# A whole two-block network on one core: raw first products, moved side work, more expert buffers, and constant products in TensorE's waits

## The reference, cut to what matters

```python
# first block (x: 512 x 1024)
h = rms_norm(x, norm_mix)
proj = h @ w_in                                # 1024 -> about 15,600 columns, split for four branches and their gates
ys = [mamba2_branch(...), rglru_branch(...), retention_branch(...), rwkv7_branch(...)]
merged = sum(sigmoid(gate_m) * (ys[m] @ w_branch[m]) for m in range(4))
x = x + merged @ w_out
h = rms_norm(x, norm_ffn)
u = causal_dwconv(h @ ffn_up)                  # 1024 -> 2 * 2816
x = rms_norm(x + (silu(gt) * val) @ ffn_down, norm_final)
# second block: modulated norms of x and of a context (256 tokens), with six vectors from c @ w_mod
#   gated delta net in both directions + neighbourhood attention, one input and one output projection
#   x = x + gate1 * (concat(gdn, attention) @ w_out_2)
# 16 experts, each takes the 64 tokens with the highest router score:
p = softmax(modulated(rms_norm(x)) @ w_router)
for e in range(16):
    tok = top_64(p[:, e])
    y_e = (silu(h[tok] @ w_gate[e]) * (h[tok] @ w_up[e])) @ w_down[e]    # three 1024 x 1024 matrices
    x[tok] += gate2 * p[tok, e] * y_e
out = rms_norm(x, final_norm_2)
```

## Time and profile before

| | us |
|---|---|
| median of 3 runs | 3022.27 (3018.67 to 3022.57) |
| the profiled execution | 3020.42 |
| its span in the trace | 3018.6 |
| PE busy | 2852.8 (95%) |
| DVE, ACT, POOL busy | 1529.3, 674.6, 713.0 |
| granted TensorE clock, mean | 0.983 of full |

### The profile page before, as it was taken

The page is one execution under the profiler, slowest core; times in us unless marked ns, Lnnn a source line. Parts: engine busy times, 40 slices in busy tenths (PEclk is TensorE's granted clock), DMA queues, the critical chain, the costliest instruction groups (busy, mean ns, idle before and its releaser), DMA issues. The chain is left out here.

```text
span 3018.6 us, 53749 instructions
## 1 busy us (share of the span) xinstructions
PE 2852.8 (95%) x22652; PEld 2048.3 (68%) x22652; DVE 1529.3 (51%) x2561; ACT 674.6 (22%) x1196; POOL 713.0 (24%) x523
## 2 busy tenths in 40 slices
PE   9999999998999989899999999999889997999998
PEld 5854866896788578758688888677768744443432
DVE  5765737445655567645577753764555322111112
ACT  2133022003333334311111100321454211110111
POOL 1212122110888346412122100111257300000000
PEclk9999999999999999999999999999999998999999
DMA  4243223331667100033222223233200047999996
GB/s 171 84 144 105 87 78 112 99 94 59 209 239 256 39 11 4 4 136 92 84 84 84 84 77 91 91 95 91 67 20 4 23 175 283 378 409 409 409 409 266
DMA packets 128477, 426.83 MB, mean 141 GB/s; under 512 B 14945, under 2 KB 22753, under 8 KB 127985
## 3 DMA queue, kind: packets, MB, share of 16 engines
q1 hardware_dynamic: 125936, 412.92, 38.8%
q0 software_dynamic: 2304, 10.49, 1.0%
HBM read 414.09 MB, written 5.06 MB: 139 GB/s over the span
## 5 line engine op out<-in xcount | busy, mean ns | idle before, releaser
L960 PE MATMUL ps<-arena 128*128 128x256 f32 x5376 | 1179.4, 381 | 18.1 <-PEq L911 6.8
L960 PEld LDWEIGHTS ps<-arena 128*128 128x128 f32 x5376 | 1016.3, 191 | 189.2 <-issue 34.7
L891 POOL TENSOR_TENSOR arena<-arena 128x512 f32<-128x512 f32 x90 | 122.4, 1360 | 629.5 <-DMA arena<-in_w_in 293.7
L897 POOL TENSOR_TENSOR arena<-arena 128x512 f32<-128x512 f32 x90 | 114.7, 1274 | 552.7 <-PE ps L960 552.7
L1111 ACT ACTIVATE arena<-ps 128x256 f32<-128x256 f32 x96 | 36.7, 382 | 890.0 <-PE ps L960 507.6
L4200 PE MATMUL ps<-arena 128*64 128x512 f32 x1024 | 224.7, 594 | 10.8 <-DMA arena<-in_w_up 8.4
L1193 DVE SCALAR_TENSOR_TENSOR arena<-ps,params,arena 128x511 f32<-128x511 f32 (+4 forms) x266 | 190.6, 717 | 15.6 <-ACT arena L1094 6.5
L1268 DVE TENSOR_TENSOR arena<-ps,arena 128x256 f32<-128x256 f32 x96 | 40.7, 424 | 300.2 <-PE ps L960 296.3
L4200 PEld LDWEIGHTS ps<-arena 128*64 128x64 f32 x1024 | 83.8, 137 | 150.2 <-issue 149.7
L4309 DVE TENSOR_TENSOR arena<-arena,ps 128x512 f32<-128x512 f32 x16 | 10.3, 683 | 294.7 <-ACT arena L4260 294.7
L1624 POOL TENSOR_TENSOR arena<-arena 128x1024 f32<-128x1024 f32 x56 | 147.7, 2638 | 8.7 <-ACT arena L1609 3.4
(11 more groups left out here) (462 smaller groups left out, 3908.1 us busy)
## 6 DMA issues: line engine op xcount, KB each, us to landing
arena<-in_w_in SPq DMA_DIRECT2D x166, 512.0 KB, 4.2
arena<-in_w_gate SPq DMA_DIRECT2D x128, 512.0 KB, 15.5
arena<-in_w_up SPq DMA_DIRECT2D x128, 512.0 KB, 15.2
arena<-in_w_down SPq DMA_DIRECT2D x128, 512.0 KB, 15.4
arena<-in_w_mod SPq DMA_DIRECT2D x64, 512.0 KB, 4.6
arena<-in_ffn_up SPq DMA_DIRECT2D x44, 512.0 KB, 4.1
arena<-in_w_branch SPq DMA_DIRECT2D x32, 512.0 KB, 3.8
arena<-spill POOLq DMA_DIRECT2D x16, 640.0 KB, 5.3
```

Of the source, the lines that this page charges most:

```text
L891: vec.tensor_tensor(plane(u, n), part(u, 1, 0), part(u, 1, 1), ALU.add).then_inc(sem, 1)
L897: vec.tensor_tensor(plane(u, n), part(u, 0, 0), part(u, 1, 0), ALU.subtract).then_inc(sem, 1)
L960: last = nc.tensor.matmul(k.bank(b)[:, 0:HT], lhs[:, q * P:(q + 1) * P], rhs[:, q, :], start=(first and q == 0), stop=(q == 3), skip_group ...
```

## The change

Neutral list of the edits, then the core of the diff.

1. **Start and first merge norm** get `lead=2`. DVE multiplies the raw planes by the norm's weight in place, as soon as they are squared; the first two C units use these planes, with the sums of squares (`strips`, `close`) between their products; DVE multiplies by the root when it evicts the two units, and makes the normed planes for the later units after the root. At the start the narrow projection `w_dt` moves from unit 1 to unit 2, the first weight piece is loaded right behind x, and the norm's weights are loaded on their own behind x's first plane.
2. **ModSide** begins one unit later and spreads its 64 steps over 17 units. (`max(u, 0)`, `UNITS - 1`)
3. **ContextNorm**: its 8 products move from job 18 to the end of the phase, its roots, scales and shifts into the ffn's down phase.
4. **Folds** of the second block's projections move from units 16 and 17 to 17 and 18.
5. **gdn_phase** does output tile 1's half product too, at block 0 beat 6 on PE, evicted by DVE at block 1 beat 2; the later phase has four products less.
6. **Five more spare slots** for the experts, in the constants from `sel` on, which are used up by then. 24 spare slots, 34 in all.
7. **Last pair's w_down** comes in column halves: 32 pieces of 256 KB, first all of the low half, then the high one; ACT copies the low half out while PE multiplies the high one.
8. **hold**: products of the constants `ones` and the first 512 constants, which nobody reads, in these places: 5 and 2 (257 columns) around the first strips at the start; 3 at the retention's end; 2 at the end of the last merge; 3 at the start of the ffn's projections; 2 behind the context's sums; 2 at the end of the second block's projections; 1 before and 1 behind HeadNorm's products; in the choice of tokens 1, 1 and 9; with the first pair of experts 2 before and 1 behind the turn.
9. The semaphores used so far are given back once more, cleared by POOL at the end of the retention's projections.

```diff
+    def hold(self, n, bank, width=T):
+        for _ in range(n):
+            self.nc.tensor.matmul(self.bank(bank)[:, 0:width], self.const("ones"), self.cst[:, 0:width], start=True, stop=True, skip_group_check=True)
@@ fast_phase, tensor
+            k.hold(held, 6)
             if ahead is not None:
                 ahead.pe(pe)
+                if lead and ui == lead:
+                    for c in range(KT):
+                        pe.wait_ge(*ahead.ready_at(c))
-                                if ahead.ready_at(q)[1]:
+                                if lead:
+                                    ahead.between(pe, q)
+                                    pe.wait_ge(*ahead.raw_at(q))
+                                elif ahead.ready_at(q)[1]:
                                     pe.wait_ge(*ahead.ready_at(q))
+                            x = ahead.src(q) if ui < lead else j["rhs"](q)
@@ fast_phase, vector, finish
                         nc.vector.tensor_tensor(dst, src, j["gate"], ALU.mult).then_inc(k.dve_evac, 1)
+                        if i < lead:
+                            dve.wait_ge(*j["evac"])
+                            link(nc.vector.tensor_tensor(dst, dst, ahead.rt, ALU.mult))
+                elif i < lead:
+                    nc.vector.tensor_tensor(dst, src, ahead.rt, ALU.mult).then_inc(k.dve_evac, 1)
@@ Norm
+    sums_at = (1, 3, 5)          # FirstNorm: (None, 0, 2)
+    def between(self, pe, q):
+        if q == self.sums_at[0]:
+            self.strips(pe, 3)
+        if q == self.sums_at[1]:
+            self.strips(pe, 7)
+        if q == self.sums_at[2]:
+            self.close(pe)
     def dve(self, dve):
+        if self.lead:
+            for c in range(KT):
+                dve.wait_ge(self.squared, self.base * KT + c + 1)
+                nc.vector.tensor_scalar(self.src(c), self.src(c), self.weight(c), None, ALU.mult).then_inc(self.k.raw_ready, 1)
+            dve.wait_ge(self.root, self.base + 1)
+            dve.wait_ge(*self.raw_at(KT - 1))
+            for c in range(KT):
+                nc.vector.tensor_tensor(self.dst(c), self.src(c), self.rt, ALU.mult).then_inc(self.ready, 1)
+            return
@@ ModSide
-        return min(self.steps, -(-self.steps * (u + 1) // self.UNITS))
+        return min(self.steps, -(-self.steps * max(u, 0) // (self.UNITS - 1)))
@@ ContextNorm
+    def sums(self, pe):
+        for c in range(KT):
+            pe.wait_ge(self.squared, c + 1)
+            ins = self.k.nc.tensor.matmul(self.k.bank(7)[:, 0:CTX], self.k.const("ones"), self.sq(c), start=(c == 0), stop=(c == KT - 1))
+        ins.then_inc(self.summed, 1)
+        self.k.hold(2, 6)
@@ gdn_phase, tensor
+                    if (b, beat) == (0, 6):
+                        pe.wait_ge(first_in, 16)
+                        for kq in range(4):
+                            ins = nc.tensor.matmul(k.bank(FIRST_BANK), first_plane[:, kq * P:(kq + 1) * P], pl(y + 4 + kq), start=(kq == 0), stop=(kq == 3))
@@ route_phase, tensor
             ins.then_inc(c_ok, 1)
+            k.hold(1, 0)
             pe.wait_ge(m_ok, 1)
...
             ins.then_inc(l_ok, 1)
+            k.hold(1, 0)
             pe.wait_ge(a_ok, 1)
...
+            k.hold(9, 3)
             pe.wait_ge(s_ok, 1)
@@ experts_phase, tensor
+                if p == 0:
+                    k.hold(2, 5)
                 turn(p)
+                if p == 0:
+                    k.hold(1, 5)
@@ experts_phase, scalar
-                nc.scalar.activation(Y[:, 0:512], k.bank(6), ACT.Copy)
+                low = nc.scalar.activation(Y[:, 0:512], k.bank(6), ACT.Copy)
+                if p == PAIRS - 1:
+                    low.then_inc(y_out, 1)
+                    act.wait_ge(y_ok, PAIRS + 1)
@@ second_block
-                       folds=[(16, 18, ab[:, 0:4, :]), (17, 19, ab[:, 4:6, :])]),
+                       folds=[(17, 18, ab[:, 0:4, :]), (18, 19, ab[:, 4:6, :])]),
+    used_up = CONST_AT["sel"]
+    spare = [pl(n, 2) for n in spare] + [k.cst[:, used_up + 2 * T * n:used_up + 2 * T * (n + 1)] for n in range(5)]
```

More of the change, by code:

```diff
@@ L338, in project_phase @@
 def project_phase(k, jobs, following=(), beside=None, moves=(), ahead=None, side=None, halves=None, afterwards=None, tail=None, loads=None, mods=None,
-                  moves_after=None):
+                  moves_after=None, held=0, at_end=None):
     if halves is not None:
-        return fast_phase(k, jobs, halves, following, beside, moves, ahead, afterwards, tail, side, mods, moves_after)
+        return fast_phase(k, jobs, halves, following, beside, moves, ahead, afterwards, tail, side, mods, moves_after, held, at_end)
     nc = k.nc
@@ L552, in down_pieces, with down_phase @@
     return [jobs[c + m]["pieces"][p][0] for c in range(0, len(jobs), 2) for p in range(len(jobs[0]["pieces"])) for m in range(2)]
-def down_phase(k, jobs, planes, turned, sums, copies, following=(), beside=None, tail=None):
+def down_phase(k, jobs, planes, turned, sums, copies, following=(), beside=None, tail=None, side=None):
     nc = k.nc
@@ L679, in _ @@
         def _(act):
+            if side is not None:
+                side.roots(act)
             for u in range(PAIRS_):
+                if side is not None and u == 2:
+                    side.shifts(act)
                 act.wait_ge(*product(NP * u + NP - 1, "P2"))
@@ L747, in _ @@
             for s in range(STEPS + 1):
+                if side is not None and s == NP + 2:
+                    side.scales(dve)
                 if s < NP:
@@ L785, in sum_plane, with fast_phase @@
         return self.k.pl(self.sums[(4 * s + n) % len(self.sums)])
-def fast_phase(k, jobs, h, following=(), beside=None, moves=(), ahead=None, afterwards=None, tail=None, side=None, mods=None, moves_after=None):
+def fast_phase(k, jobs, h, following=(), beside=None, moves=(), ahead=None, afterwards=None, tail=None, side=None, mods=None, moves_after=None, held=0,
+               at_end=None):
     nc = k.nc
@@ L800, in fast_phase @@
     assert all(len(j["pieces"]) == 1 for j in jobs)
+    lead = ahead.lead if isinstance(ahead, Norm) else 0
+    assert all(u[0] == "C" for u in h.units[:lead])
     np_ = len(pieces)
@@ L1050, in _ @@
                     tail.add(pe, c)
+            if at_end is not None:
+                at_end(pe)
         @block.scalar
@@ L1379, in pe @@
     def pe(self, pe):
-        for c in range(0 if self.early else KT):
+        for c in range(0 if self.early or self.lead else KT):
             self.add(pe, c)
@@ L1424, in pe @@
         k = self.k
+        k.hold(1, 7)
         for c in range(4):
@@ L1447, with pe @@
 class FirstNorm(Norm):
+    sums_at = (None, 0, 2)
+    def pe(self, pe):
+        pe.wait_ge(self.ones_in, 16)
+        self.k.hold(5, 6, self.near)
+        self.strips(pe, 3)
+        self.k.hold(2, 6, self.near)
     def begin(self):
@@ L2160, in _ @@
                 squares(2 * m + 1)
+            k.hold(3, 0)
         @block.vector
@@ L3367, in silu_done, with gdn_phase @@
         return self.jobs[i]["post_n"]
-def gdn_phase(k, q, kv, ctx_kv, cp, y, planes, late, fills):
+def gdn_phase(k, q, kv, ctx_kv, cp, y, planes, late, first, fills):
     nc = k.nc
@@ L3499, in _ @@
         def _(sp):
+            sp.dma_start(first_plane, first[0]).then_inc(first_in, 16)
             sp.wait_ge(xv_ok, 2 * 4 + 2)
@@ L4231, in _ @@
                         gates(p + 1)
+                pe.wait_ge(k.piece_done, g)
+                nc.tensor.nop().then_inc(y_ok, 1)
+            for f in range(2):
+                for q in range(8):
+                    for e in range(2):
+                        pe.wait_ge(*loaded(g))
+                        nc.tensor.matmul(k.bank(6 + f)[64 * e:64 * e + 64, :], HT[:, q * P + 64 * e:q * P + 64 * e + 64], slot(g)[:, 0:512],
+                                         start=(q == 0), stop=(q == 7)).then_inc(k.piece_done, 1)
+                        g += 1
                 pe.wait_ge(k.piece_done, g)
@@ L4380, in order @@
         zs = tiles(W_Z, 8, z, func=ACT.Silu)
+        zs[:2] = [job(wtile(dr["w_in"], W_Z + i), H, "D", pl(z + i), post=silu) for i in range(2)]
+        start.first_piece = zs[0]["pieces"][0][0]
         js = zs[:2] + convs(W_XBC, 16, xs, "ssm_conv_w", "ssm_conv_b", 4, silu, nch=16) + zs[2:]
-        js.insert(1, job([(dr["w_dt"], 0, 8)], H, "A", pl(WORK + 26), strips=True))
+        js.insert(2, job([(dr["w_dt"], 0, 8)], H, "A", pl(WORK + 26), strips=True))
         plan(k, project_phase, k, js, beside=rest_of_consts(k), ahead=start,
              halves=halved(paired(25, lead=3), [H_PL], [WORK + 46], [WORK + 54 + n for n in range(8)] + [WORK + 24],
-                           folds=[(9, 1, k.small[:, 0:64].rearrange("p (i h) -> p i h", h=16))]))
+                           folds=[(9, 2, k.small[:, 0:64].rearrange("p (i h) -> p i h", h=16))]))
         gates = [w + 22 + n for n in range(5)] + [bt, ct, bt + 1]
@@ L4446, in order @@
         js += [branch3(c, raw=gate3(c)) for c in range(KT)]
```

(2 more changed lines are left out.)

117 lines of the change are left out of this document (72 added, 45 removed).

## The result

The changed kernel takes 2987.53 us (median of 4 runs, 2982.9 to 2989.94) where the kernel before takes 3022.42 (3018.67 to 3022.94): a ratio of 0.9885, interval 0.9868 to 0.9902, 35 us less. On another occasion it had 2987.55 against 3018.43, 31 less. Forecast were 2974, 46 to 48 less, in a range of 2963 to 2991. The forecast range holds the time, the likeliest case's own range (2966 to 2984) does not. The profiled execution took 2989.94, the longest of the four, with a mean granted clock of 0.991, where before it was 0.983.

The account below looks back on a forecast made before the run. PE's own stream, gaps and half clock were taken to bound the kernel up to the experts, which end by the DMA. Savings summed to 46.1 us: 3020.4 - 46.1 = 2974.3, own range 2966 to 2984, widened by rivals to 2963 to 2991.

Parts of the forecast that it names:

- Start: Kernel start: the first two units and `w_dt` end at 29.8 instead of 35.35, less 0.3 for a load: 5.2 us saved.
- ModSide: Behind the retention: PE's wait in the second unit goes (6.3) and full clock follows (2.5): 8.8 us saved.
- Ffn and context norm: Ffn's norm: holds keep full clock, 3.0 us saved; context norm: products moved and clock kept in the down phase, 5.9.
- HeadNorm and the moved product: Phase behind gdn: two holds in HeadNorm save 1.4 us, four products leaving for gdn save 3.5.
- Experts: Experts' phase: five more slots save 6.4 us, the first pair's holds 1.7, the last pair's split copies 1.3.
- The last pair's halves: Last experts' w_down: the copies of 1.30 us go behind the high half, saving 1.3.
- Folds: Second block's projections: the gap moves behind unit 17, keeping 4.3 us and its slow stretch: 0 saved (-0.5 to 6.5).
- Choice of tokens: Router stage: first hold delays scores by 0.6 us, nine holds speed the gathers by 2.4: 1.8 saved (-3 to 2.4).
- Gdn: Output tile 1's half product moved into gdn's gap: DVE's eviction costs 0.4 us, steps behind the gap save 1.7.
- First merge norm: First merge: the two units end at 282.5 instead of 287.0: 4.6 us saved, bounds 2.5 and 5.5.
- Rwkv core: Rwkv core: no term in the prediction, so 0 us of change.
- A: Rival at the holds: the constants don't hold the clock, losing 15.2 us plus 2 for overhangs: 2991.5; chance 12%.

Follow-up runs that it names:

- folds_7: The changed kernel with the second fold in PSUM bank 7, a bank for each fold: 2981.99 us, 5.6 below the changed kernel.
- merge_hold: The changed kernel with two products of constants in the gap at the start of the first merge: 2985.29 us, 2.3 below the changed kernel.
- no_holds: The changed kernel without any of the constant products: 2988.02 us, against 2987.55 for the changed kernel.

## Why the prediction was right, and where it fell short

What held, step by step. *Start*: 4.7 and 5.4 for 5.2. *ModSide*: 8.1 and 8.5 for 8.8; alone 6.5, for the 6.3 of waits. *Ffn and context norm*: 8.6 for 8.9. *HeadNorm and the moved product*: 4.4 for 4.9. *Experts*: 8.7 and 8.5 for 9.4, of which the slots 6.2 for 6.4, and the first pair's holds 1.8 for 1.7. The last pair's halves gave less than their 1.3: the copy's gap of 1.30 is one of 0.40 now, but the down products take 14.4 instead of 13.96, so 0.5 is left. By the fit of the Trainium skill (DMA: Bandwidth & Descriptors, section "Anatomy of one DMA — SWDGE (gpsimd) path"; it is given for transfers that GpSimd issues, and here SP issues them) the halves would have come 12 us late, an estimate. The trace does not agree: the last pair's down products wait for no transfer. (2974.3 and 12 are 2986, not the 2984 of the prediction.) *Folds*: the gap moved and kept its size and its slow unit, as worked out, and folds_7 shows its cause and its price: 5.4 to 6.9 in the stage, 3.6 with the stage behind it.

What failed. 46.1 less 30.3 is 15.8, and four places make 13 of it.

*Choice of tokens*: 1.8 forecast, -2.3 came (both profiles, with the gathers). The step that failed is "the first hold delays the scores by 0.6": it put a full-clock price on a hold in a stretch where the clock falls (1.38, not 0.87), and had the scores behind it at full clock. The scores began 5.9 behind the norm's close, not 4.7, and took 1.73, not 1.04. From the close to the gathers the five profiles with that hold have 26.7 to 27.9, the nine without it 24.8 to 25.7. The lower bound of -3 covered it. Its second half, that nine holds save the gathers' clock, needed the wait filled to 0.4 us; nine left 2.2.

*Gdn*: 1.3 forecast, -2.5 to -4.4 came. The term "the steps behind the gap run at half clock now: +1.7" gave 0.7 (the gap ends where it did, 8.1 behind the phase's first product, for DVE's chain sets it). The rest is half clock late in the phase (1.6 and 3.0) and 0.6 to 1.5 of PE's waits for issue more. Gdn is as long in the two changed kernels without the moved product, so the loss is not the product's; what sets it stays open.

*First merge norm*: 4.6 forecast, 1.2 to 2.9 came. The sequence was right, but it had no term for the clock behind its own gap of 2.6, and the range "2.5 and 5.5" named DVE, not this. merge_hold gives 4.5. (By the prediction's own numbers, 287.0 less 282.5, the term is 4.5.) It also took the earlier trace rows for the rule, where two of four profiles of before's own first merge are 1.8 to 2.2 longer.

*Rwkv core*: 0 forecast, -1.4 to -2.0 came. This may be chance, and the profiles don't tell more: between two profiles of the kernel before the same stage with its start differs by 1, among all with that core by 6.

Of the rivals, A was the nearest by its number (2991.5) and is wrong by its mechanism: the holds kept the clock everywhere but in the choice of tokens. That the range held the time is therefore in part luck: its upper end of 2991 was A's, and the losses that brought the time near it are others. The forecast summed 14 small terms, each from rows, and took for granted that what it did not touch would run as in the one profiled execution; its own range of 18 us had no term for that. Repaired in three places and held in two more the kernel reaches 2972, where the forecast put the change as it stood.

## What to carry to other kernels

Read the stages of two or more executions at the same instructions before pricing changes of 1 or 2 us, of the kernel before too: here a stage without any edit, the rwkv core's, took 325.7 to 331.3 in four profiles before and 327.4 to 335.1 in ten after. Fill a wait of the matrix engine with idle products only where nothing queues behind them, and fill it to under a microsecond (here that kept the clock in all but one case, with a further gap of 1.55 behind it, and leaving 2.2 us did not); a product ahead of something on the chain costs its slow price, not its fast one. Where moving an operation only moves its gap, ask which buffer ties it to the other: the second fold needed another bank, not another place. And look at the next gap when one is closed: behind the closed fold the next one lost the clock and took back some of the gain.

## What the runs showed of the hardware

The clock behind a gap is not a matter of the gap alone: 2.42 us cost nothing in one execution and 1.7 in another of the same kernel, 2.63 cost 1.5 or more in each profile without a hold, 1.55 behind a filled wait cost 1.6 in one of four profiles, and late in gdn half clock came behind 0.94. The granted clock was 0.50 there, the lower level, after a stretch in which PE had run small products with short waits:

```profile
2401.26 2.08 PE L3726 MATMUL ps<-arena 64*128 64x128 f32 x16 [0.94 <-DVE arena L3929]
2403.27 3.78 PE L3783 MATMUL ps<-arena 128*128 128x512 f32 x4
```

Idle products that nobody reads, 0.44 us a matmul of 512 columns at full clock, kept it in each of the places where they filled the gap to less than 1 us and no further gap followed. PE's waits without a releaser ("issue") sum up to between 4.6 and 9.4 us in the rwkv core. They are not all chance: in each of the 14 profiles two of the larger ones, of 1.0 to 2.1 and of 0.8 to 1.7, lie 72 to 76 and 101 to 105 us behind the core's first product. They are at L2453 in the nine changed kernels with holds, and at L2461 in no_holds, which is L2385 in the four kernels with the core as before. Others move or come and go. What ties these two to their place is not shown.
